# Fox's output projection ahead of MLA attention, its weights split during fox attention, two experts loaded during MLA, and the second part accumulated in steps

## The reference, cut to what matters

```python
o_fox = blocked_causal_attention(fq, fk, fv, cum)      # 8 heads of 64
o_mla = blocked_causal_attention(q, k, mv)             # 8 heads of 64, q and k of 96
mix = concatenate([rmsnorm(o_fox, g_fox_out), rmsnorm(o_mla, g_mla_out)])   # 512 + 512
h = h + mix @ w_o                                      # w_o: 1024 x 1024
u = rmsnorm(h, g_ffn)
# group logits -> one of 4 groups; expert logits -> two of its 8 experts, with weights
for e in range(32):
    y = y + combine[:, e:e+1] * ((silu(u @ w1[e]) * (u @ w3[e])) @ w2[e])
return (h + y)[meta tokens dropped]
```

## Time and profile before

| what | value |
|---|---|
| median of three runs | 628.41 us |
| profiled execution, in all | 628.14 us |
| profiled execution, from the first to the last instruction | 626.4 us |
| mean granted TensorE clock | 0.988 |
| TensorE matmul / weight load busy | 94% / 65% |
| VectorE, ScalarE, GpSimd busy | 42%, 37%, 22% |
| moved by the DMA engines | 141.64 MB, 226 GB/s in the mean |

### The profile page before, as it was taken

How to read it: one execution, slowest core, us unless ns; L and a number is a source line. 1 busy time by engine, 2 the same in 40 slices (tenths; PEclk the granted TensorE clock), 3 DMA queues, 4 the chain that set the end, 5 groups by cost and what they waited for, 6 DMA issues and landing times.

```text
span 626.4 us, 9256 instructions
## 1 busy us (share of the span) xinstructions
PE 587.5 (94%) x3559; PEld 408.1 (65%) x3559; DVE 265.6 (42%) x603; ACT 233.8 (37%) x445; POOL 140.9 (22%) x233
## 2 busy tenths in 40 slices
PE   8899999998999989999989999999999997877896
PEld 8778788786775447666778766566566554554554
DVE  3644245554484988437745771111111111101217
ACT  6826516543555473456616522212122121111220
POOL 6300001150233412122510011332322322212200
PEclk9999799999999989999989999999999999999999
DMA  8930000006400053000199499999999999999995
GB/s 274 335 121 1 0 2 0 1 2 239 182 1 0 34 235 135 10 1 1 30 427 413 146 412 370 372 397 379 395 393 384 389 398 393 394 395 391 398 378 216
DMA packets 32941, 141.64 MB, mean 226 GB/s; under 512 B 8689, under 2 KB 10785, under 8 KB 19841
## 3 DMA queue, kind: packets, MB, share of 16 engines
q1 hardware_dynamic: 26016, 127.02, 52.3%
q0 software_dynamic: 6304, 11.93, 5.8%
q10 hardware_dynamic: 576, 2.10, 0.8%
HBM read 132.85 MB, written 16.06 MB: 238 GB/s over the span
## 4 chain that ended last, share of the span: by engine, by line
PE 82%; DVE 10%; issue 4%; ACT 3%; POOL 1%; DVEq 0%; ACTq 0%; POOLq 0%
PE ps L2314 18%; PE ps L1953 16%; PE ps L2345 10%; PE ps L2149 6%; PE ps L2272 5%; PE ps L2032 4%; PE ps L2138 3%; PE ps L2087 3%; PE ps L2330 2%; PE ps L2107 2%; PE ps L1917 2%; DVE sums_s L1703 1%; PE ps L1926 1%; DVE x L1864 1%; PE ps L2193 1%
## 5 line engine op out<-in xcount | busy, mean ns | idle before, releaser
L2314 PE MATMUL ps<-w,xt 128*64 128x256 f32 x1024 | 116.6, 380 | 15.3 <-issue 15.0
L2314 PEld LDWEIGHTS ps<-w,xt 128*64 128x64 f32 x1024 | 76.9, 137 | 61.7 <-issue 33.0
L1633 DVE TENSOR_TENSOR xt<-ps,g_ffn_c 128x512 f32<-128x512 f32 x32 | 22.0, 692 | 187.1 <-PE ps L2272 187.1
L2345 PE MATMUL ps<-w,hT 128*64 128x512 f32 x256 | 61.8, 604 | 0.0
L1290 ACT ACTIVATE hsb<-ps,row_scale 128x256 f32<-128x256 f32 x32 | 15.2, 475 | 113.8 <-PE ps L2314 113.8
L917 POOL DMA_INDIRECT xg<-h_rows,idx x30 | 28.8, 960 | 109.0 <-PE ps L2272 108.6
L909 POOL DMA_INDIRECT y_rows<-yh,idy x29 | 29.5, 1016 | 65.3 <-ACT yh L1312 62.4
L2149 PE MATMUL ps<-probT,vals 128*128 128x512 f32 (+4 forms) x160 | 42.7, 411 | 1.0 <-POOL probT L846 1.0
L1714 DVE TENSOR_REDUCE nmax<-ps 128x1 bf16<-128x528 f32 (+1 forms) x64 | 28.0, 502 | 35.9 <-PE ps L2108 35.9
L846 POOL TENSOR_SCALAR_AFFINE_SELECT probT<-probT 128x128 f32<-128x128 f32 (+2 forms) x80 | 21.2, 288 | 83.8 <-ACT probT L1202 82.5
L2272 PEld LDWEIGHTS ps<-ident,xg 64*128 64x128 f32 x256 | 30.2, 200 | 11.6 <-issue 11.5
(11 more groups left out here) (353 smaller groups left out, 1061.8 us busy)
## 6 DMA issues: line engine op xcount, KB each, us to landing
w<-in_w SPq DMA_DIRECT2D x96, 1024.0 KB
x<-in_x SPq DMA_DIRECT2D x8, 512.0 KB, 9.5
y_rows<-zeros POOLq DMA_DIRECT2D x1, 4096.0 KB, 12.3
yg<-y_rows SPq DMA_DIRECT2D x4, 1024.0 KB, 11.0
w_in_v<-in_w_in SPq DMA_DIRECT2D x1, 2048.0 KB, 11.0
w_in_k<-in_w_in SPq DMA_DIRECT2D x1, 2048.0 KB, 16.8
w_in_q<-in_w_in SPq DMA_DIRECT2D x1, 2048.0 KB, 21.6
w_oa<-in_w_o SPq DMA_DIRECT2D x1, 2048.0 KB, 10.2
```

The lines of the kernel that those rows point to most:

```text
L2314: ins = pe.matmul(ps[j * slots:(j + 1) * slots, 2 + b, 0:F], xt[b][:, k, :], w13[s][:, j, k, :], start=(k == 0), stop=(k == DK - 1))
L2345: ins = pe.matmul(ps[q * slots:(q + 1) * slots, 6 + b, :], hT[b][:, m, :], w2s[s][:, m, q * 512:(q + 1) * 512], start=(m == 0), stop=(m == ...
```

## The change

Fox's weight chunks 0 to 3 are split behind the fox heads 3, 4, 5 and 7 (`WEIGHT_AT`), and VectorE makes their low parts at heads 4 and 6 and in unit 2 (`LOW_AT`). The high parts now lie where `qS` lies, in parts that are free by then. Group 0 gets banks of its own (`FOX_BANKS`), so that p = 0, 1 and 2 are projected whole before MLA attention and p = 3 among MLA's first maxima; `add_fox` of 0 to 2 stands ahead of `attend(1)`. Group 1 of tiles 0 and 1 is accumulated in steps of one or two chunks, tile 0's first two at heads 14 and 15. Tiles 2 and 3 follow among the transposes and routers of tiles 0 and 1, so that the projections no longer alternate with every router; four `keep_warm` matmuls of each of three tiles go. Experts 0, 1 and w1 of 6 are loaded when group 0 is done, in other slots than before, and w2 of 5 when the mixed output is normalised.

```diff
-        slot_at = [r_qk, r_qk + SLOT, ring + SLOT, ring + 2 * SLOT, ring + 3 * SLOT, ring]
+        slot_at = [ring + SLOT, ring + 2 * SLOT, r_qk, r_qk + SLOT, ring + 3 * SLOT, ring]
...
-        wo_hi = [place(f"wo_hi{b}", [P, HALF_K, D], F32R, ring + SLOT * (1 - b)) for b in range(2)]
+        wo_hi = [place(f"wo_hi{b}", [P, HALF_K, D], F32R, ring + narrow * (1 - b)) for b in range(2)]
...
-        WEIGHT_AT = {H + 3: 4, H + 4: 6, GS - 2: 5, GS - 1: 7}
-        WEIGHT_ORDER = [0, 1, 2, 3] + list(WEIGHT_AT.values())
+        WEIGHT_AT = {3: 0, 4: 1, 5: 2, H - 1: 3, H + 3: 4, H + 4: 6, GS - 2: 5, GS - 1: 7}
+        WEIGHT_ORDER = list(WEIGHT_AT.values())
+        LOW_AT = {4: (0,), 6: (1, 2), H + 4: (4,), H + 6: (6,), GS - 1: (5,)}
...
-        WO_BANKS, TURN_U2, LOGITS, RANKS, INDEX, COUNT = (4, 0), 2, 6, 7, 4, 5
+        WO_BANKS, FOX_BANKS = (4, 0), (4, 2, 0, 0)
+        TURN_U2, LOGITS, RANKS, INDEX, COUNT = 2, 6, 7, 4, 5
...
+            sp.wait_ge(wo_done, NT)
+            sp.wait_ge(y_zeroed, 16)
+            load_expert(0, 0)
+            load_expert(1, 1)
+            sp.dma_start(w13[6][:, 0, :, :], w1_v[6]).then_inc(w13_in[6], 16)
             sp.wait_ge(scored, 3 * GS)
             sp.wait_ge(pv_done, GS)
-            load_expert(0, 0)
-            load_expert(1, 1)
-            sp.wait_ge(wo_done, NT)
-            sp.wait_ge(y_zeroed, 16)
             load_expert(2, 2)
             load_expert(3, 3)
-            sp.dma_start(w13[6][:, 0, :, :], w1_v[6]).then_inc(w13_in[6], 16)
+            sp.wait_ge(o_done, DK)
+            sp.dma_start(w2s[5][:, :, :], w2_v[5]).then_inc(w2_in[5], 16)
             sp.wait_ge(wo_done, 2 * NT)
-            sp.dma_start(w13[4][:, 0, :, :], w1_v[4]).then_inc(w13_in[4], 16)
-            sp.dma_start(w13[4][:, 1, :, :], w3_v[4]).then_inc(w13_in[4], 16)
-            load_expert(5, 5)
+            for s in (4, 5):
+                sp.dma_start(w13[s][:, 0, :, :], w1_v[s]).then_inc(w13_in[s], 16)
+                sp.dma_start(w13[s][:, 1, :, :], w3_v[s]).then_inc(w13_in[s], 16)
...
                 if 2 <= n < 2 + HALF_K:
-                    split_weight(n - 2)
                     split_mix(n - 2)
...
             invert_mix(0)
             add_fox(0)
+            add_fox(1)
+            add_fox(2)
             attend(1)
...
             mix_low(DK - 1)
-            add_fox(2)
-            add_fox(3)
             invert_mix(1)
             add_mla(0)
+            add_mla(1)
             for p in range(1, NT):
...
                 choose_group(p - 1)
-                if p == LAST:
-                    add_mla(p)
                 choose_experts(p - 1)
                 if p < LAST:
-                    add_mla(p)
+                    add_mla(p + 1)
...
                 score_maxes(g0)
                 if ph == 1:
-                    out_project(1, 0, 1)
+                    out_project(3, 0, 0)
                 score_maxes(g0 + 1)
-                keep_warm(OUT, 0 if ph else 3)
+                if ph == 1:
+                    out_project(3, 0, 1)
...
                 if ph == 1:
-                    pe.wait_ge(fox_added, 2)
+                    pe.wait_ge(fox_added, NT)
...
-                    elif g == GS - 2:
-                        out_project(2, 0, 0)
+                    elif g >= GS - 2:
+                        out_project(0, 1, 0, (g - GS + 2,))
+                        out_project(0, 1, 1, (g - GS + 2,))
...
                     out_project(0, 0, 0)
                     out_project(0, 0, 1)
+                else:
+                    out_project(1, 0, 0)
+                    out_project(1, 0, 1)
                 turn_up(n)
-            out_project(1, 0, 0)
+            out_project(2, 0, 0)
+            out_project(2, 0, 1)
...
-            out_project(2, 0, 1)
-            out_project(3, 0, 0)
-            out_project(3, 0, 1)
-            sum_totals(1)
-            out_project(0, 1, 0)
-            out_project(0, 1, 1)
-            for p in range(1, NT):
+            for q in range(2):
+                out_project(1, 1, q, (0, 1))
+            for p in range(2):
+                for q in range(2):
+                    out_project(p, 1, q, (2,))
+            for p in range(2):
+                for q in range(2):
+                    out_project(p, 1, q, (HALF_K - 1,))
+                if p == 0:
+                    sum_totals(1)
+            for p in range(2, NT):
+                turn_u2(p - 2)
+                if p >= 3:
+                    ranks(p - 3)
                 out_project(p, 1, 0)
-                turn_u2(p - 1)
-                if p >= 2:
-                    ranks(p - 2)
-                keep_warm(WO_BANKS[p % 2] + 1, 4)
-                router(p - 1)
+                router(p - 2)
                 out_project(p, 1, 1)
-            keep_warm(COUNT, 5)
-            turn_u2(LAST)
-            ranks(LAST - 1)
-            router(LAST)
+            for p in range(NT - 2, NT):
+                if p == LAST:
+                    keep_warm(COUNT, 5)
+                turn_u2(p)
+                ranks(p - 1)
+                router(p)
```

More of the change, by code:

```diff
@@ L289, in build @@
         probT = [place(f"probT{b}", [P, 3, 512], F32, r_p + 6144 * b) for b in range(2)]
-        sums_at = [ring + 2 * SLOT - 2 * SEQ * 4, ring + narrow]
+        sums_at = [ring + 2 * SLOT - 2 * SEQ * 4, ring + SLOT - 2 * SEQ * 4]
         sums_s = [place(f"sums_s{b}", [P, SEQ], F32, sums_at[b // 2] + SEQ * 4 * (b % 2)) for b in range(4)]
@@ L1175, in split_weight @@
                 act.wait_ge(wo_in[c // HALF_K], 16)
+                if c == 0:
+                    act.wait_ge(late_in, LATE * 16)
                 if c in FREED_BY:
@@ L1539, in add_fox @@
                 dve.wait_ge(tile_in[i], 32)
-                dve.scalar_tensor_tensor(out=x[:, i, :], in0=pair(WO_BANKS[p % 2], D), scalar=mix_rinv[:, i:i + 1],
+                dve.scalar_tensor_tensor(out=x[:, i, :], in0=pair(FOX_BANKS[p], D), scalar=mix_rinv[:, i:i + 1],
                                          in1=x[:, i, :], op0=ALU.mult, op1=ALU.add).then_inc(fox_added, 1)
@@ L1717, in attend @@
                 row_maxes(g0)
+                row_maxes(g0 + 1)
                 if ph == 1:
-                    add_fox(1)
-                row_maxes(g0 + 1)
+                    add_fox(3)
                 for g in range(g0, g0 + H):
@@ L1729, in attend @@
                         normalise(g // 2 - 1, [g % 2])
[L1730 to L1733, removed]
+                    for c in LOW_AT.get(g, ()):
+                        weight_low(c)
+                    if g == GS - 3:
+                        mix_low(HALF_K)
+                    if g == GS - 1:
+                        mix_low(HALF_K + 1)
             attend(0)
@@ L1739, in _ @@
                     normalise(H // 2 - 1)
+                if n == 2:
+                    weight_low(HALF_K - 1)
                 if 2 <= n < 2 + HALF_K:
-                    weight_low(n - 2)
                     mix_low(n - 2)
@@ L2005, in sum_totals, with out_project @@
                 ins.then_inc(sq_totals, 1)
-            def out_project(p, group, q):
+            def out_project(p, group, q, chunks=tuple(range(HALF_K))):
                 i = TILE_ORDER[p]
-                bank = WO_BANKS[p % 2]
-                pe.wait_ge(wo_hi_made, (group + 1) * HALF_K)
-                pe.wait_ge(mix_hi_made, (group + 1) * HALF_K)
-                pe.wait_ge(wo_lo_made, (group + 1) * HALF_K)
-                pe.wait_ge(mix_lo_made, (group + 1) * HALF_K)
+                bank = WO_BANKS[p % 2] if group else FOX_BANKS[p]
+                last = group * HALF_K + chunks[-1]
+                pe.wait_ge(wo_hi_made, max(WEIGHT_ORDER.index(group * HALF_K + c) for c in chunks) + 1)
+                pe.wait_ge(mix_hi_made, last + 1)
+                pe.wait_ge(wo_lo_made, max(WEIGHT_ORDER.index(group * HALF_K + c) for c in chunks) + 1)
+                pe.wait_ge(mix_lo_made, last + 1)
                 if group:
@@ L2022, in out_project @@
                         pe.wait_ge(mix_rooted, 1)
-                elif p == 1:
-                    pe.wait_ge(up_staged, NU)
-                elif p == 2:
-                    pe.wait_ge(maxed, NT * GS)
+                elif p < 3:
+                    pe.wait_ge(up_staged, NU - 2 + p)
                 else:
-                    pe.wait_ge(exped, 3 * GS)
+                    pe.wait_ge(fox_added, 3)
                 m_hi, m_lo, w_hi_o, w_lo_o = mix_hi[group], mix_lo[group], wo_hi[group], wo_lo[group]
                 for n, (m, w) in enumerate(((m_hi, w_hi_o), (m_lo, w_hi_o), (m_hi, w_lo_o))):
-                    for k in range(HALF_K):
+                    for k in chunks:
                         ins = pe.matmul(ps[:, bank + q, :], m[:, k, i * P:(i + 1) * P],
@@ L2034, in out_project @@
                                         stop=(n == 2 and k == HALF_K - 1))
-                if q == 1:
+                if q == 1 and chunks[-1] == HALF_K - 1:
                     ins.then_inc(wo_done, 1)
```

9 lines of the change are left out of this document (6 added, 3 removed).

## The result

The changed kernel takes **634.31 us** (median of 4 runs, 632.62 to 634.78) against 627.84 us (four runs, 626.17 to 628.76) for the kernel before on the same chip: a ratio of 1.0102, 95% interval 1.0079 to 1.0125. It is slower by 6.5 us, or 1.0%. I had predicted 632.0 (625.9 to 635.0) with a chance of 0.63 for slower: right in sign and inside the range, 2.3 us too low. (The interval excludes 1, so slower is clear of the noise.)

A forecast was written before the change was run, and what follows sets the result against it. The end was taken to follow expert 0's start, behind a serial chain. Terms 10.7 + 0.5 - 5.1 - 1.5 - 0.8 = +3.8 us on the profiled execution gave 631.9, taken as 632.0 us (range 625.9 to 635.0).

The forecast's parts named there:

- What bounds the kernel: Expert loop: one unbroken weight stream from slot 0's release, so the kernel's end follows the start of expert 0.
- wrong in kind: Sign against the bound: TensorE's waits in the expert loop shrink by several us, instead of about 0.8 us in sum.
- Part 1: Weight split moved into fox attention: zero at unit 3's transposes (224.10 us), +1.05 and -1.05 us cancelling.
- port: Rival in the up-projections: mix_low(0) isn't stretched, half clock at 224 us goes too; 628.8 us, no change; chance 0.16.
- Part 2: Fox's projection ahead of MLA: +10.7 us to the first MLA score, including waits for add_fox.
- Part 3: MLA's last heads: no more work, but head 15's products wait for weight_low(5) and mix_low(5); +0.5 us (0 to 1.3).
- Part 4: From the last MLA head's end (T) to add_mla(0): T+13.1 instead of T+18.2, -5.1 us, with 1.2 charged for half speed.
- Part 5: Routing stage: order -2.6 us, half clock behind gaps at routers 2 and 3 +1.1; -1.5 us (-2.6 to +1).
- slower: Rival, MLA's tail and routers: head 15 +0.8, half-speed first-token products +1.5, ScalarE's chain +0.7; 635.0 us; chance 0.15.
- Part 6: Early loads of experts 0, 1 and half of 6: -0.8 us and no more, as slot 0's release bounds expert 7.
- Faster: the clock: Rival: TensorE at full speed at 225 us, after the last head and at routers; 626.5 us and below; chance 0.14.
- Doesn't load early: Rival on expert loads: SyncE's wait or a slot delays them; only the 0.8 us is missing; no chance of its own.

The follow-up runs named there:

- experiment 5: Changed kernel plus 22 warming matmuls (4.8 us) ahead of the transposes of expert 0's gathered rows: 639.41 us, ratio 1.0189.
- experiment 10: Kernel before plus 8 warming matmuls in the gap before unit 3's transposes: 627.73 us, ratio 0.9997.
- Experiment 4: Changed kernel with fox's projection of position 3 back behind MLA, experts 0, 1 and w1 of 6 loaded behind the last head: 629.19 us, ratio 1.0021.
- experiment 1: Changed kernel plus 18 warming matmuls: 9 before router(2), 6 before ranks(2), 3 before router(3): 630.75 us, ratio 1.006.
- experiment 7: Changed kernel plus 12 warming matmuls before chunk 3's projection and 9, 6 and 3 in the routers' gaps: 628.87 us, ratio 1.0024.
- experiment 2: Changed kernel plus 12 warming matmuls between the products of chunk 2 and chunk 3, behind the last head: 631.64 us, ratio 1.0064.
- experiment 3: Changed kernel with the loads of experts 0, 1 and half of 6 issued behind the last MLA head again: 633.66 us, ratio 1.0096.
- experiment 8: Changed kernel plus 9 warming matmuls before router(2) alone, later gaps left: 634.23 us, ratio 1.0102.
- experiment 9: Changed kernel with fox's position 3 behind MLA, routers' gaps filled, and 8 more warming matmuls before unit 3's transposes: 627.58 us, ratio 1.0.

## Why the prediction was right in sign and low by 2.3 us

It is 2.3 us low between the medians, and 3.0 (+6.8 against +3.8) between the two profiles. One term missed by more than that, and smaller ones made up for part of it.

**What bounds the kernel: right.** The end follows the start of expert 0: 4.8 us of warming ahead of it moved the end by 5.1 between the medians (experiment 5), and across all twelve traces the time from expert 0's product to the end lies between 251.5 and 253.8 us, while its start lies between 371.4 and 384.9. One sign that I had set for being wrong in kind did show: the waits of TensorE in the loop shrank by several us, from 15.0 to 10.4, not by 0.8. Before, and below it after:

```profile
L2314 PE MATMUL ps<-w,xt 128*64 128x256 f32 x1024 | 116.6, 380 | 15.3 <-issue 15.0
```

```profile
L2334 PE MATMUL ps<-w,xt 128*64 128x256 f32 x1024 | 119.9, 388 | 10.7 <-issue 10.4
```

The experts' first products took 3.3 us longer in the same loop, some of them at half clock, and filled that much of the waits; waits and products together are 131.9 and 130.6 us. The kernel before does the same in another execution (experiment 10: 121.6 us of work, 10.5 of waits). So the sign was badly chosen, since it can't tell a shorter wait from slower work, and the bound stands.

**Part 1: right, zero.** Unit 3's transposes moved by 1.10 us with everything ahead of them (unit 0's went from 206.53 to 207.65, the matmuls at 69 us by 1.13). The row of VectorE and GpSimd came out as in before:

```profile
219.18 2.18 DVE L1536 TENSOR_TENSOR mix_lo<-mixT,mix_hi 128x512 fp32r<-128x512 f32 x1
219.47 1.12 POOL L834 CAST qTb<-qT 97x1024 bf16<-97x1024 f32 x1
```

The rival "port" fell. VectorE began 0.29 us ahead of the cast, to the hundredth as in before, and again was the one stretched. It ended 0.77 us behind the cast, about the 0.69 us of its kin, as if it had waited for the cast to end. The rule of the Trainium skill, "SBUF — State Buffer", section "SBUF: two separate sides", by which the first to start holds the shared port pair for its whole instruction, would have had the cast wait; by the starts in the trace this row does not agree with it, for the second time. The profile's times of GpSimd are rough, so 0.29 us is a weak measure of who was first.

**Part 2: right.** 10.6 us against 10.7. The first wait for add_fox, put at 0.6, is 0.61; the second, put at 0.45 over the present wait of 0.23, is 0.53, that is 0.30 over it. Experiment 4 bears on the price by taking one position back: 4.9 us for 24 matmuls of 5.5 us and 0.9 us of waits, of which 1.6 us stood over another wait.

**Part 3: right.** Head 15's products wait 0.86 us for mix_low(5), inside my 0.4 to 1.5; +0.7 in all against +0.5.

**Part 4: right.** -4.9 against -5.1. The gap was 3.05 us against 3.3; half clock behind it cost 1.4 us (T+13.3 against T+11.9 with the gap filled) against the 1.2 that I charged.

**Part 5: the step that failed.** I put -2.6 for the order and **+1.1 for half clock**. The order was right: 44.65 - 2.6 is 42.05, and with the gaps filled the stretch takes 42.5 (experiment 1) and 41.5 (experiment 7). The clock's term measured 634.31 - 630.75 = **3.6 us** between the medians, and 47.35 - 42.5 = 4.9 in the profile, which is the dearest of the profiles with this order (46.5 and 45.7 us in experiments 2 and 3: 4.0 and 3.2). The mechanism stood in my text, and so did the gaps: 2.6 us forecast ahead of router(2), 2.02 measured; 2.8 ahead of router(3), 1.88 and 0.63 with full clock before them (experiment 8), while in after the slowed work fills all but 0.61. I sized it by the wrong neighbour. Behind the gap at 225 us stand dense products, which were slow for one group of twelve, 1.7 us; I charged about two thirds of that. In the routing stage the work behind a gap is thin: 36-column router matmuls with more idle time among them, and the clock stayed at half for 17 us, until 373.7, right through the heavy products of the first tokens (+2.6 us on eight of them). That those would be reached stood among the rivals ("slower", +1.5 for them, 635.0, chance 0.15). It was the likelier case (all six profiles with an unfilled gap there have it: 4.65 to 6.28 us instead of 3.65) and belonged in the forecast; with it the sum would have been 632.0 + 1.5 + 0.7 = 634.2.

The argument by which I made the charge small, that a gap of 2.20 us in the expert loop is followed by full clock, doesn't hold either. After has both kinds, behind gaps of the same length (TensorE in the loop, in time):

```profile
539.69 3.67 PE L2334 MATMUL ps<-w,xt 128*64 128x256 f32 x32 [2.25 <-issue]
...
557.49 5.36 PE L2334 MATMUL ps<-w,xt 128*64 128x256 f32 x32 [2.25 <-issue]
```

One full-clock neighbour was no bound. There the fall costs nothing that shows, as the weight stream sets the pace: after has it and needs 251.6 us from expert 0's product to the end, before has full clock at the gaps that I read and needs 253.2.

**Part 6: right in kind.** Forecast -0.8; -1.6 between the two traces from expert 0 to the end, of which putting the loads back accounts for 0.9, while the medians show none of it. The DMA engines were idle for 13.3 us ahead of slot 0's release (some 10 forecast). An earlier load can't pass the ring's first release.

**The rivals.** "Faster: the clock" did not happen by itself, and filling the gaps behind MLA (experiment 7) shows its size: 628.9, not 626.5. Its share at 225 us was not filled there, and filling it brought no gain (experiments 9 and 10). "Doesn't load early": it does, and it matters as little as said.

## What to carry over

Before moving work ahead of a bound stage, ask what shade it has now: the same 24 matmuls cost 0.3 us behind MLA (1.7 against a gap filled otherwise), under VectorE's normalisation, and 4.9 us in front of it. Before taking filler matmuls or independent products out of a thin stage, price the clock for the whole stage up to the next dense products, not for one group: here 3.6 us between the medians (3.2 to 4.9 in the profiles), more than the order's own gain of 2.1. Filling all gaps up to the heavy work won the clock back; filling the first one alone gained nothing that four runs can show, and the last ones alone were not tried.

## What the runs showed of the hardware that I had not expected

- The clock stayed at half through a stretch in which the trace has TensorE busy for 15.39 of 16 us (clock 0.53, 356 to 372 us of after). Adding 18 warming matmuls (4 us of work) made the kernel 3.6 us faster.
- The same gap (2.02 us ahead of router(2)) had different prices: 2.80, 3.60, 2.63 and 2.74 us for the router behind it in after and experiments 2, 3 and 5, and 1.96 us in variant 4, where the fall came only behind the router. From add_mla(0) to expert 0's product it was 47.35, 46.5 and 45.7 us in after, 2 and 3 and 43.2 in variant 4, so a single profile doesn't tell the price.
- A slow stretch from 20 to 40 us and one at 225 us excluded each other in ten of ten profiles. A gain or a loss of 1 to 2 us in one stretch between two single profiles may be one half of such a pair and no effect of the edit.
